# Two moves in the order of one feed-forward pair: the norm's root later on VectorE, the last quarter's turn sooner on TensorE

## The chip, the core and the metric

The kernel runs on one core of a Trainium2 chip. A core has five engines that run beside each other and meet at semaphores: TensorE (PE, and PEld for its weight loads), VectorE (DVE), ScalarE (ACT), GpSimd (POOL) and SyncE (SP), which here only issues DMA. The metric is the device time of one execution in microseconds (us). The median of three runs is 2067.35 us (2067.28 to 2067.61).

## The reference

Two transformer layers stand one behind the other, on 256 rows of width 2048, all in fp32. The change touches the second layer only, where the mixers end and the feed-forward begins:

```python
y = _rms(h, norm_mix_g[i])
z = y @ w_in[i]
...
h = h + jnp.concatenate([oa, ob, oc, od], axis=-1) @ w_out[i]
y = _rms(h, norm_ffn_g[i])
h = h + (jax.nn.silu(y @ w_gate[i]) * (y @ w_up[i])) @ w_down[i]
```

`_rms(x, g)` is `x * rsqrt(mean(x*x) + 1e-6) * g` over a row. The row's factor commutes with the product by the weights, so the kernel multiplies by the gains g first and applies the factor to the sums that come out. The factor is "the norm's root" of this text. D_FF is 5632, which makes 11 blocks of 512 columns of w_gate and w_up, taken as 11 pairs.

## The kernel before, in words

**Products.** Every fp32 matrix is split in a high and a low part, and each product is three matmuls, high by high, low by high, high by low (L714, L715 and L716 in `three`). A *unit* is a block of weights of 128x2048: SyncE loads it to a `raw` buffer, ScalarE copies it to the high part `hi` (L1252, `split`), VectorE makes the low part `lo` by a subtraction (L1721, `split`), and TensorE multiplies. ScalarE and VectorE split unit u + 3 while TensorE is at unit u (AHEAD = 3). There are four `hi` buffers, so ScalarE's split of unit u waits until TensorE has done unit u - 4.

**Residual.** X is the residual stream. The product by w_out of the second layer is four groups, `out2` 0 to 3, each of four units and each for one quarter of X's 512 columns. When a group is done VectorE adds it to its quarter (L2304), ScalarE takes the quarter's sums of squares (L1280 and L1281, counted by `ss3_made`), and TensorE turns the quarter by 8 transposes (L979, `flip`, called by `turn_h`). Of the turned quarter ScalarE writes the high part with the gains (L1268, `high`, four activations) and VectorE the low part (L1822, `low`, four operations). At which unit all this is done for quarter f is said by the table TURN2, which all three engines read.

**The first pair.** The units behind out2 are those of the feed-forward. A pair of 512 columns is done by a scheme with 7 block products for 8 (Strassen's, in Winograd's form), in 11 steps, one unit each, in the order a, x, p2, f, p3, e, d, p0, c, g, p1. BEGIN[0] is the number of the first pair's step a. Steps a, x, f, e, d, c and g are 12 matmuls with 512 columns, and p2, p3, p0 and p1 are 24. The weights of x, f, g and e are no loads: VectorE makes them by subtraction from the loaded blocks (L1738, in `mixed`). Step p2 needs the third quarter turned (`flip_low` to SECOND + 3), and step p3 the last (SECOND + 4). Three rules of order matter here:

- TensorE does the side work of a unit before the unit's matmuls, in order of the program. A transpose that waits holds up all matmuls behind it. The turn of quarter 3 waits for `bank_dve`, which VectorE raises when L2304 of group out2 3 is done.
- VectorE at unit u does first the side work of u (the low part of a turned quarter, the root), then the form and the low part of unit u + 3, then what ends unit u.
- ScalarE at unit u does the side work of u, then the high part of unit u + 3, then what ends unit u; at a step x the copy of a sum (L1504) stands before the high part.

**The root.** From the sums of squares VectorE makes the factor for both halves of the rows: one reduction (L1714), mean and epsilon (L1711), an integer start value (L1688, L1689), three Newton steps of three operations (L1691 to L1693), and two more operations (L2208, L2209) that raise `ffn_scales`. That is 15 operations on 128x2 numbers, each waiting for the one before it. Its first reader is ScalarE's tanh at step p0 (L1526), which waits for `ffn_scales` and for a sum that VectorE adds at the end of step d (L1764, L1766).

Of the kernel before, what the change touches and what calls it, by code (L numbers as in the profile page):

```python
# [241 lines left out]
def build_hybrid(nc, A, C, out, scratch):  # L242
    with ExitStack() as ctx:
# [281 lines left out]
        def freed(name):  # L525

            return named[name].freed
# [35 lines left out]
        OUT, MIXERS, OUT2 = [named[n].first for n in (("out", 0), ("cf", 0), ("out2", 0))]  # L563
# [2 lines left out]
        LAST_GATES = named["gs", GATES - 1].first  # L566
        MERGE = {LAST_GATES + 3: 0, LAST_GATES + 5: 1, OUT: 2, OUT + 1: 3}
        TURN1 = {OUT + 6 + 4 * f: f for f in range(4)}
        TURN2 = {OUT2 + 6 + 4 * f: f for f in range(4)}
        BEGIN = [named["S", j].first for j in range(11)]  # L570
        LAST_DOWN = 4 * LAST_TURN
        TURN3 = {named["down", LAST_DOWN + f].last + 2: f for f in range(4)}
# [43 lines left out]
        def scale_cols(gcol, f):  # L616
            return [VC[:, gcol + 4 * f + k:gcol + 4 * f + k + 1] for k in range(4)]
# [94 lines left out]
        def tensor_program(e):  # L712
# [407 lines left out]
            def turn_h(n, f):  # L1120
                e.wait_ge(flip_low, n)
                flip(lambda t, k: X[:, t, 512 * f + 128 * k:512 * f + 128 * k + 128], 1)
# [12 lines left out]
            def channel_sum(dst, src, counted):  # L1135
                for c in range(4):
                    x = e.matmul(dst, ONE, src[:, c, :], start=c == 0, stop=c == 3)
                x.then_inc(counted, 1)

            def side(u):  # L1140
# [50 lines left out]
                if u == MIXERS + 28:  # L1191
                    e.wait_ge(cv_squared, 1)
                    channel_sum(psB[:, 0, 512:768], CB, channels_summed)
                if u in TURN2:
                    e.wait_ge(bank_dve, freed(("out2", TURN2[u])))
                    turn_h(SECOND + TURN2[u], TURN2[u])
                if u == P_TURN:
# [35 lines left out]
        def scalar_program(e):  # L1233
# [26 lines left out]
            def high(n, dst, pair, scale):  # L1260

                ps = c4(psB[:, pair, :])
                e.wait_ge(flip_turned, turned(n))
                if isinstance(scale, float):
                    e.activation(dst, ps, ACT.Copy, scale=scale).then_inc(flip_high, 1)
                else:
                    for k in range(4):
                        x = e.activation(dst[:, k, :], ps[:, k, :], ACT.Copy, scale=scale[k])  # L1268
                    x.then_inc(flip_high, 1)
# [83 lines left out]
            def part_high(src, block, scale):  # L1353
                e.activation(YH[block], src, ACT.Copy, scale=scale).then_inc(mix_high, 1)

            def side(u):
# [105 lines left out]
                if u == MIXERS + 30:  # L1462
                    e.wait_ge(cn_made, 1)
                    part_high(CA[:, :, :], 2, 0.5)
                if u in TURN2:
                    f = TURN2[u]
                    high(SECOND + f, XH[:, 4 * f:4 * f + 4, :], 1, scale_cols(32, f))
# [209 lines left out]
        def vector_program(e):  # L1677
            steps = [0]

            def finish(x):  # L1680

                steps[0] += 1
                x.then_inc(dve_step, 1)
                e.wait_ge(dve_step, steps[0])

            def rsqrt(v, y, w):
                yi = y.bitcast(I32)
                finish(e.tensor_scalar(yi, v.bitcast(I32), 1, None, ALU.logical_shift_right))  # L1688
                finish(e.tensor_scalar(yi, yi, -1.0, float(0x5F3759DF), ALU.mult, ALU.add))  # L1689
                for _ in range(3):  # L1690
                    finish(e.tensor_tensor(w, y, y, ALU.mult))  # L1691
                    finish(e.scalar_tensor_tensor(out=w, in0=w, scalar=-0.5, in1=v, op0=ALU.mult, op1=ALU.mult))
                    finish(e.scalar_tensor_tensor(out=y, in0=w, scalar=1.5, in1=y, op0=ALU.add, op1=ALU.mult))  # L1693
# [16 lines left out]
            def mean_eps(v, n):  # L1710
                finish(e.tensor_scalar(v, v, 1.0 / n, EPS, ALU.mult, ALU.add))  # L1711

            def row_sums(src, dst):
                finish(e.tensor_reduce(dst, src.rearrange("p (t f) -> p t f", t=2), AX.X, ALU.add))  # L1714
# [98 lines left out]
            def low(n, dst, dstH, pair, scale):  # L1813

                ps, dH = c4(psB[:, pair, :]), dstH.bitcast(F32)
                e.wait_ge(flip_high, n + 1)
                if isinstance(scale, float):
                    e.scalar_tensor_tensor(out=dst, in0=ps, scalar=scale, in1=dH, op0=ALU.mult,
                                           op1=ALU.subtract).then_inc(flip_low, 1)
                else:  # L1820
                    for k in range(4):
                        x = e.scalar_tensor_tensor(out=dst[:, k, :], in0=ps[:, k, :], scalar=scale[k], in1=dH[:, k, :],  # L1822
                                                   op0=ALU.mult, op1=ALU.subtract)
                    x.then_inc(flip_low, 1)
# [219 lines left out]
            def part_low(src, block, scale, n):  # L2044
                e.wait_ge(mix_high, n)
                e.scalar_tensor_tensor(out=YL[block], in0=src, scalar=scale,
                                       in1=YH[block].bitcast(F32), op0=ALU.mult,
                                       op1=ALU.subtract).then_inc(mix_low, 1)
# [20 lines left out]
            def side(u):  # L2069
# [48 lines left out]
                if u in MERGE:  # L2118
                    f = MERGE[u]
# [5 lines left out]
                if u in TURN1:  # L2125
                    f = TURN1[u]
# [63 lines left out]
                if u == MIXERS + 30:  # L2190
# [8 lines left out]
                    part_low(CA[:, :, :], 2, 0.5, 3)  # L2199
                if u in TURN2:  # L2200
                    f = TURN2[u]
                    low(SECOND + f, XL[:, 4 * f:4 * f + 4, :], XH[:, 4 * f:4 * f + 4, :], 1, scale_cols(32, f))
                if u == BEGIN[0] + 3:
                    e.wait_ge(ss3_made, 4)
                    row_sums(ss3, v2)
                    mean_eps(v2, 2048)
                    rsqrt(v2, rr_, w2_)
                    finish(e.tensor_scalar(hr2, rr_, 0.5, None, ALU.mult))  # L2208
                    e.tensor_tensor(r2h, hr2, rr_, ALU.mult).then_inc(ffn_scales, 1)  # L2209
# [10 lines left out]
                if u in TURN3:  # L2220
                    f = TURN3[u]
# [113 lines left out]
            for u in range(n_units):  # L2335
                side(u)
                g, i = units[u]
                if u in ENDED:
                    ended(ENDED[u])
                if 0 < u < n_units - AHEAD:  # L2340
                    if units[u + AHEAD][0].kind == "S":
                        mixed(u + AHEAD)
                    else:
                        split(u + AHEAD)
                if u == GATE_SUMS:
                    e.wait_ge(flip_turned, turned(3))
                    input_forms(GXT, GSS)
                if u == SUMS:
                    e.wait_ge(flip_low, SECOND + 2)
                    input_forms(XT, SS)  # L2350
                if u in FORMS_LOW:
                    forms_low(FORMS_LOW[u])
                if g.kind == "S":
                    gate_up(u)
                elif u == g.last:
                    post(g)
# [95 lines left out]
```

## Time and profile before

| | us |
|---|---|
| median of 3 runs | 2067.35 |
| lowest, highest | 2067.28, 2067.61 |
| the profiled execution | 2066.91 |
| its span, first to last instruction | 2064.8 |
| TensorE busy | 2045.4 (99%) |
| VectorE busy | 1567.9 (76%) |
| ScalarE busy | 1040.9 (50%) |
| granted TensorE clock over the span | 0.998 |

The profiled execution is 2.1 us longer than its span, and 0.4 us under the median. A timeline view has one line for each instruction or row of equal ones: start, duration, engine, line, operation, tiles; in brackets how long the engine had stood idle before it and what released it. Durations on TensorE overlap, since its matmuls are pipelined; what a matmul costs in a row of them is the distance between two starts. The same holds by about 0.08 us for VectorE and ScalarE. In a view of stretches each engine's busy time is followed by its count of instructions; the number behind POOL's is the granted clock, 1.00 for 2.4 GHz and 0.50 for 1.2 GHz.

### The profile page before, as it was taken

The numbers are of one execution on the slowest core, as the hardware profiler recorded it, in microseconds if no ns is written. First come the engines' busy times: TensorE is split into PE (matmuls) and PEld (weight loads), VectorE is DVE, ScalarE is ACT, GpSimd is POOL, SyncE is SP. The second block draws the span as 40 slices with busy tenths as digits, with TensorE's granted clock in tenths as the row PEclk, the third lists the DMA queues.
The fourth block names the chain that finished last, engine by engine and source line by source line (L and its number), as shares of the span: only waits on it lengthen the run. The fifth ranks groups of instructions, "written<-read, shape, count | busy, mean of one in ns | idle before, by whom it ended". The sixth has DMA issues, their size and how long they took to land.

```text
span 2064.8 us, 24955 instructions
## 1 busy us (share of the span) xinstructions
PE 2045.4 (99%) x10311; PEld 1739.1 (84%) x10311; DVE 1567.9 (76%) x1461; ACT 1040.9 (50%) x982; POOL 99.3 (5%) x200
## 2 busy tenths in 40 slices
PE   9999999999999999999999999999999999999998
PEld 8888888888888888888999987888888888888887
DVE  6576555765688888855789859989888889888565
ACT  6444443544455555545344445645455545555453
POOL 2000000000000000000000000111110011110000
PEclk9999999999999999999999999999999999999999
DMA  8655555555565655655655566666566666666461
GB/s 252 215 183 175 166 169 184 164 183 178 189 211 204 222 203 184 219 204 183 210 184 165 182 204 209 230 213 194 192 220 227 211 207 194 201 225 224 145 234 59
DMA packets 229857, 403.61 MB, mean 195 GB/s; under 512 B 13763, under 2 KB 59067, under 8 KB 229489
## 3 DMA queue, kind: packets, MB, share of 16 engines
q1 hardware_dynamic: 221344, 387.64, 56.7%
q0 software_dynamic: 7648, 13.26, 2.2%
q8 instruction: 82, 1.34, 0.3%
q10 hardware_dynamic: 752, 1.12, 0.2%
q14 instruction: 31, 0.25, 0.0%
HBM read 394.62 MB, written 2.12 MB: 192 GB/s over the span
## 4 chain that ended last, share of the span: by engine, by line
PE 89%; DVE 8%; ACT 1%; issue 1%; DMA 1%; ACTq 0%; SPq 0%; DVEq 0%
PE psA L714 20%; PE psA L716 20%; PE psA L715 20%; PE psA L921 6%; PE psB L714 5%; PE psB L715 5%; PE psB L716 5%; PE psA L925 3%; DVE lo L1721 3%; DVE CA L2031 1%; DVE raw L1738 1%; PE psB L979 1%; ACT hi L1252 1%; DVE lo in Y L1721 1%; DMA X<-in_x_dram 0%
## 5 line engine op out<-in xcount | busy, mean ns | idle before, releaser
L1721 DVE TENSOR_TENSOR lo<-raw,hi 128x2048 fp32r<-128x2048 f32 (+2 forms) x364 | 822.7, 2268 | 262.5 <-ACT hi L1252 260.7
L1252 ACT ACTIVATE hi<-raw 128x2048 fp32r<-128x2048 f32 (+2 forms) x364 | 689.2, 1899 | 456.3 <-PE psA L716 300.2
L714 PE MATMUL psA<-hi,XHL 128*128 128x512 f32 x1008 | 393.8, 391 | 1.7 <-DVE XHL L1822 1.7
L716 PE MATMUL psA<-hi,XHL 128*128 128x512 f32 x1008 | 390.9, 388 | 0.0
L715 PE MATMUL psA<-lo,XHL 128*128 128x512 f32 (+1 forms) x872 | 337.7, 387 | 0.0
L714 PE MATMUL psA<-hi,YHL 128*128 128x512 f32 x624 | 244.3, 392 | 0.0
L716 PE MATMUL psA<-hi,YHL 128*128 128x512 f32 x624 | 243.0, 389 | 0.0
L714 PEld LDWEIGHTS psA<-hi,XHL 128*128 128x128 f32 x1008 | 189.4, 188 | 40.9 <-issue 2.1
L716 PEld LDWEIGHTS psA<-hi,XHL 128*128 128x128 f32 x1008 | 189.3, 188 | 39.2
L715 PE MATMUL psA<-lo,YHL 128*128 128x512 f32 x536 | 208.6, 389 | 0.0
L715 PEld LDWEIGHTS psA<-lo,XHL 128*128 128x128 f32 x872 | 163.9, 188 | 32.2
L714 PE MATMUL psA<-XHL,hi 128*128 128x256 f32 (+1 forms) x528 | 150.2, 284 | 1.5 <-DVE lo L1867 1.5
L715 PE MATMUL psA<-XHL,hi 128*128 128x256 f32 (+1 forms) x528 | 149.3, 283 | 0.0
L716 PE MATMUL psA<-XHL,lo 128*128 128x256 f32 (+1 forms) x528 | 149.3, 283 | 0.0
L1252 ACT ACTIVATE hi<-raw in Y 128x2048 fp32r<-128x2048 f32 x55 | 105.5, 1918 | 78.5 <-PE psA L716 48.8
L1721 DVE TENSOR_TENSOR lo in Y<-raw in Y,hi 128x2048 fp32r<-128x2048 f32 x55 | 125.8, 2288 | 24.1 <-ACT hi L1252 23.9
L921 PE MATMUL psA<-XHL,hi 128*128 128x512 f32 x576 | 138.6, 393 | 0.0
L716 PEld LDWEIGHTS psA<-hi,YHL 128*128 128x128 f32 x624 | 117.1, 188 | 24.5
L714 PEld LDWEIGHTS psA<-hi,YHL 128*128 128x128 f32 x624 | 117.2, 188 | 23.9 <-issue 0.3
L921 PEld LDWEIGHTS psA<-XHL,hi 128*128 128x128 f32 x576 | 105.9, 188 | 21.5 <-issue 0.6
L715 PEld LDWEIGHTS psA<-lo,YHL 128*128 128x128 f32 x536 | 100.7, 188 | 20.5
L714 PE MATMUL psB<-hi,XHL 128*128 128x512 f32 (+1 forms) x300 | 115.4, 385 | 1.8 <-DVE lo in Y L1721 1.4
(435 smaller groups left out, 2891.6 us busy)
## 6 DMA issues: line engine op xcount, KB each, us to landing
raw<-in_w_in_dram SPq DMA_DIRECT2D x149, 1024.0 KB, 5.1
raw<-in_w_up_dram SPq DMA_DIRECT2D x35, 1024.0 KB, 5.2
raw<-in_w_gate_dram SPq DMA_DIRECT2D x35, 1024.0 KB, 5.2
raw<-in_w_out_dram SPq DMA_DIRECT2D x32, 1024.0 KB, 5.1
raw<-in_w_down_dram SPq DMA_DIRECT2D x32, 1024.0 KB, 5.1
raw<-in_w_ple_gate_dram SPq DMA_DIRECT2D x14, 1024.0 KB, 5.1
raw<-in_w_branch_dram SPq DMA_DIRECT2D x13, 1024.0 KB, 5.1
raw in Y<-in_w_down_dram SPq DMA_DIRECT2D x12, 1024.0 KB, 5.1
```

Of the source, the lines that this page charges most:

```text
L714: e.matmul(dst, A2[0], B2[0], start=first, stop=False, skip_group_check=True)
L715: e.matmul(dst, A2[0], B2[1], start=False, stop=False, skip_group_check=True)
L716: return e.matmul(dst, A2[1], B2[0], start=False, stop=last, skip_group_check=True)
L921: e.matmul(both, hh[:, s], XHL[:, kb, :, :].rearrange("p a t -> p (a t)"), start=i == 0 and n < 2, stop=False, skip_group_check=True)
L925: x = e.matmul(both[:, 256:512], ll[:, s], XH[:, kb, :], start=False, stop=i == len(g.parts) - 1 and n >= 14, skip_group_check=True)
L979: x = e.transpose(ps[:, k, 128 * t:128 * t + 128], src(t, k), ID[:, :])
L1252: e.activation(hi[u % H][:, 0:m], raw[slot][:, 0:m], ACT.Copy).then_inc(hi_made, 1)
L1721: e.tensor_tensor(lo[slot][:, 0:m], raw[slot][:, 0:m], hi[u % H][:, 0:m].bitcast(F32), ALU.subtract).then_inc(lo_made, 1)
L1738: e.tensor_tensor(of[dst], of[p], of[q], ALU.subtract).then_inc(form_made, 1)
L2031: x = e.scalar_tensor_tensor(out=CA[:, c, :], in0=HP[:, c, j:j + 256], scalar=CW[:, 4 * j + c:4 * j + c + 1], in1=CA[:, c, :], op0=ALU.mul ...
```

## The change

The turn of the last quarter of X stands at unit OUT2 + 17, which is BEGIN[0] + 1 and the first pair's step x; it was at BEGIN[0] + 2, step p2. The other three quarters stay. The root stands at BEGIN[0] + 6, step d; it was at BEGIN[0] + 3, step f.

```diff
-        TURN2 = {OUT2 + 6 + 4 * f: f for f in range(4)}
+        TURN2 = {OUT2 + 6 + 4 * f - f // 3: f for f in range(4)}
...
-                if u == BEGIN[0] + 3:
+                if u == BEGIN[0] + 6:
                     e.wait_ge(ss3_made, 4)
                     row_sums(ss3, v2)
                     mean_eps(v2, 2048)
```

On VectorE, around steps a to f of the first pair. L1822 on XHL is the low part of the turned quarter, L1738 the form that step e uses, L1721 "in Y" the low part for step p3, and L1714 and L1711 begin the root:

```order
 L1721 TENSOR_TENSOR lo<-raw,hi 128x2048
-L1738 TENSOR_TENSOR raw<-raw 128x2048
-L1721 TENSOR_TENSOR lo in Y<-raw in Y,hi 128x2048
 L1822 SCALAR_TENSOR_TENSOR XHL<-psB,VC,XHL 128x256 x4
-L1721 TENSOR_TENSOR lo<-raw,hi 128x2048
+L1738 TENSOR_TENSOR raw<-raw 128x2048
+L1721 TENSOR_TENSOR lo in Y<-raw in Y,hi 128x2048
+L1721 TENSOR_TENSOR lo<-raw,hi 128x2048 x3
+L1721 TENSOR_TENSOR lo in Y<-raw in Y,hi 128x2048
 L1714 TENSOR_REDUCE SM<-SM 128x2
 L1711 TENSOR_SCALAR SM<-SM 128x2
```

The low part of the quarter moved ahead of one form and one low part of weights. Ahead of the root there stand now four low parts of weights behind p3's place (for steps e, d, p0 and c), where one stood.

The root's other end on VectorE, where L2208 and L2209 are its last two operations and L1764 begins what ends step d:

```order
 L2208 TENSOR_SCALAR SM<-SM 128x2
 L2209 TENSOR_TENSOR SM<-SM 128x2
-L1721 TENSOR_TENSOR lo<-raw,hi 128x2048 x2
-L1721 TENSOR_TENSOR lo in Y<-raw in Y,hi 128x2048
 L1721 TENSOR_TENSOR lo<-raw,hi 128x2048
 L1764 TENSOR_TENSOR CG<-CG,SU 128x512
```

The three low parts (steps d, p0 and c) that stood behind the root stand before it; the one that is left is that of step g.

On TensorE, the end of step a, step x (psB from SFH) and the start of step p2 (psA from XHL). L979 x8 is the turn of the last quarter; rows of step x between the two pieces are the same in both:

```order
 L716 MATMUL psA<-hi,XHL 128x512
+L979 MATMUL psB<-ID,X 128x128 x8
 L714 MATMUL psB<-hi,SFH 128x512
 L715 MATMUL psB<-lo,SFH 128x512
...
 L715 MATMUL psB<-lo,SFH 128x512
 L716 MATMUL psB<-hi,SFL 128x512
-L979 MATMUL psB<-ID,X 128x128 x8
 L714 MATMUL psA<-hi,XHL 128x512
 L715 MATMUL psA<-lo,XHL 128x512
```

The turn, and with it its wait for the sum of the last quarter, stands ahead of step x's 12 matmuls instead of behind them. On ScalarE the four L1268 of the quarter stand, in the same way, ahead of the copy of step x's sum (L1504) and one high part instead of behind both. GpSimd's and SyncE's orders are the same.

## Rows read from the trace of the kernel before

**Rows 1.** Chain that ended last, page part 4: share of the span by engine

```profile
PE 89%; DVE 8%; ACT 1%; issue 1%; DMA 1%; ACTq 0%; SPq 0%; DVEq 0%
```

**Rows 2.** Waits of TensorE, whole program: line <- releaser: us, times, longest

```profile
PE psA L714 <- DVE XHL L1822: 1.7, 1, 1.7
PE psB L714 <- DVE lo in Y L1721: 1.4, 2, 0.9
```

**Rows 3.** Timeline, TensorE, 1258 to 1317 us: start, us, form [idle <-releaser]

```profile
1258.44 0.39 PE L716 MATMUL psA<-hi,XHL 128*128 128x512 f32 x1
...
1258.91 0.50 PE L714 MATMUL psB<-hi,SFH 128*128 128x512 f32 x1
...
1262.43 1.09 PE L979 MATMUL psB<-ID,X 128*128 128x128 f32 x8 [0.48 <-DVE X L2304]
...
1263.28 0.47 PE L714 MATMUL psA<-hi,XHL 128*128 128x512 f32 x1
...
1265.90 0.39 PE L716 MATMUL psA<-hi,XHL 128*128 128x512 f32 x1
...
1266.72 0.50 PE L714 MATMUL psB<-hi,XHL 128*128 128x512 f32 x1 [0.43 <-ACT CG L1504]
...
1269.58 0.39 PE L714 MATMUL psA<-hi,SFH 128*128 128x512 f32 x1
...
1272.07 0.39 PE L716 MATMUL psA<-hi,SFL 128*128 128x512 f32 x1
...
1274.14 0.47 PE L714 MATMUL psA<-hi,XHL 128*128 128x512 f32 x1 [1.68 <-DVE XHL L1822]
...
1279.46 0.39 PE L716 MATMUL psB<-hi,XHL 128*128 128x512 f32 x1
...
1316.08 0.50 PE L714 MATMUL psB<-hi,XHL 128*128 128x512 f32 x1 [0.87 <-DVE lo in Y L1721]
```

**Rows 4.** Timeline, VectorE, 1260 to 1286 us

```profile
1260.98 1.40 DVE L2304 SCALAR_TENSOR_TENSOR X<-X,SM,psA 128x512 f32<-128x512 f32 x2
...
1265.73 2.29 DVE L1721 TENSOR_TENSOR lo<-raw,hi 128x2048 fp32r<-128x2048 f32 x1 [1.15 <-ACT hi L1252]
...
1267.94 2.29 DVE L1738 TENSOR_TENSOR raw<-raw 128x2048 f32<-128x2048 f32 x1
...
1272.34 1.65 DVE L1822 SCALAR_TENSOR_TENSOR XHL<-psB,VC,XHL 128x256 fp32r<-128x256 f32 x4
...
1276.11 0.15 DVE L1714 TENSOR_REDUCE SM<-SM 128x2 f32<-128x8 f32 x1
...
1278.95 4.49 DVE L1721 TENSOR_TENSOR lo<-raw,hi 128x2048 fp32r<-128x2048 f32 x2
...
1283.36 2.28 DVE L1721 TENSOR_TENSOR lo in Y<-raw in Y,hi 128x2048 fp32r<-128x2048 f32 x1
...
1285.56 2.28 DVE L1721 TENSOR_TENSOR lo<-raw,hi 128x2048 fp32r<-128x2048 f32 x1
```

**Rows 5.** Timeline, ScalarE, 1265 to 1280 us

```profile
1265.60 0.58 ACT L1497 ACTIVATE S1B<-psA 128x512 f32<-128x512 f32 x1
...
1268.36 1.57 ACT L1268 ACTIVATE XHL<-psB,VC 128x256 fp32r<-128x256 f32 x4
...
1270.26 3.71 ACT L1252 ACTIVATE hi<-raw 128x2048 fp32r<-128x2048 f32 x2 [0.34 <-DVE raw L1738]
...
1279.94 1.92 ACT L1252 ACTIVATE hi<-raw in Y 128x2048 fp32r<-128x2048 f32 x1 [3.67 <-PE psB L716]
```

**Rows 6.** Busy time per engine (instructions), clock, DMA share, GB/s; 1281 to 1315 us

```profile
1281.00:1315.00 34.00, 34.00 (x151) 27.97 (x150) 33.97 (x23) 18.35 (x14) 7.46 (x16) 1.00 0.62 203
```

**Rows 7.** The same view at the program's end

```profile
2055.00:2056.00 1.00, 0.14 (x2) 0.00 (x0) 0.26 (x1) 0.70 (x3) 0.00 (x0) 1.00 1.03 381
...
2057.00:2057.20 0.20, 0.00 (x0) 0.00 (x0) 0.01 (x1) 0.16 (x2) 0.00 (x0) 0.93 0.00 0
...
2057.20:2057.40 0.20, 0.00 (x0) 0.00 (x0) 0.17 (x2) 0.00 (x0) 0.00 (x0) 0.50 0.00 0
```
## The prediction

> **What bounds the kernel now.** I read the chain that ended last first, then TensorE's waits, then the timelines of the engines around the change. The chain is 89% TensorE and 8% VectorE [rows 1]: where TensorE runs without a gap only its own work counts, and the change adds none (the same 8 transposes, the same matmuls). So a difference can only come from the places where TensorE stands idle. Two of the waits of TensorE lie in the stretch that the change reorders [rows 2]: 1.68 us at 1274.14, before step p3, for the low part of the turned quarter, and 0.87 us at 1316.08, before step p3 of the second pair, for a low part of weights [rows 3]. Between 1274.14 and that second wait TensorE does not stop: in 1281 to 1315 both it and VectorE are busy all the time, 34.00 and 33.97 of 34 us [rows 6]. VectorE is the reason of both waits. From 1265.73 on it works back to back (a low part of weights follows another at a distance of 2.20 us: two of them fill 1278.95 to 1283.36 [rows 4]), and it is behind TensorE until 1316. Whatever stops VectorE in 1265 to 1316, or is added to it, is therefore paid by TensorE at 1316. Before 1262.4 nothing of VectorE's order changes.
>
> **The turn, one step sooner: TensorE.** The turn waits for L2304, which ends at 1260.98 + 1.40 = 1262.38 [rows 4]. Its VectorE order up to there is the same, so the turn starts at 1262.43 as before [rows 3]. Step a's last matmul starts at 1258.44; at 0.226 us a matmul (11 steps from 1269.58 to 1272.07) it makes room at 1258.67. Before, step x began at 1258.91 and filled most of the time up to the turn. Now the turn stands ahead of it, and TensorE is idle from 1258.67 to 1262.43, 3.76 us, more than twice the longest wait behind the program's start [rows 2]. Then come the turn (0.85, to 1263.28), step x's 12 matmuls (the first 12 behind a turn took 1263.28 to 1265.90 + 0.23 = 1266.13), and then p2 and f, 36 matmuls at 0.2264 = 8.15 us. So TensorE is at p3 at 1274.28. In between it waited 0.43 for ScalarE's copy of x's sum before [rows 3]; now that copy comes behind the four L1268: L1497 begins at 1265.60 and leaves ScalarE at about 1266.1, the four take 1.57, to 1267.7 [rows 5], the copy, like L1497, 0.58, to 1268.3. The second half of p2 needs it at 1266.13 + 12 x 0.2264 = 1268.85, so that wait is gone. p3 starts at 1274.28 for 1274.14: the turn's place alone gives back its own gap and costs 0.1 us, as long as the clock stays.
>
> **The turn: VectorE.** The low part of the quarter (distance 1.57 from 1272.34) and the form and the low part that change places with it (2.20 each) add up to the same: 1267.94 + 1.57 + 2.20 + 2.20 = 1273.91, as before [rows 4]. The quarter's high part, ready at 1267.7, is just in time for 1267.94. The form now ends at 1271.8 for 1270.2, and ScalarE's next high part waits for it [rows 5]: 1271.8 + 1.90 = 1273.7, 0.2 ahead of VectorE's need at 1273.91. So p3's operands are all there at 1274.0, as before, and TensorE's 1274.28 decides. The 1.68 us wait isn't saved, it has become part of the 3.76.
>
> **The root, three steps later.** Its 15 operations take 1276.11 to 1278.95, 2.84 us [rows 4]. Without it there VectorE does the low parts of d and p0 at 1276.11 and 1278.31 (their high parts: ScalarE ends them at 1273.7 + 1.86 = 1275.6 and, behind a copy, 0.58 + 1.90 later, at 1278.1) and is free at 1280.52. Next is the low part of step c. Its high part takes a buffer that step p3 holds, and ScalarE began it at 1279.94, when p3 had ended (last matmul started at 1279.46 [rows 3, 5]). Now p3 is continuous with f and its last matmul starts at 1274.28 + 23 x 0.2264 = 1279.49, so nothing has come sooner: high part 1279.97 to 1281.89, low part from 1281.91. VectorE is idle for 1281.91 - 1280.52 = 1.39 us. Before, the root stood in just this time, and c's low part began at 1283.36. Then: c's low part to 1284.11, root to 1286.95, and g's low part starts at 1286.95 for 1285.56, **1.39 us late**. From there to 1316 VectorE has no idle time in which to win it back [rows 6], and TensorE's wait there (0.87) grows by it; a part may fall one step sooner. The other reader of the root, the tanh of p0, waits for L1766 anyway, which is behind the root in either order; it gets late by the same 1.39, and its sum is used by VectorE only at step g, three TensorE steps on. SyncE's loads that wait for x, p2 and f are issued later by as much as these steps end later, x most: 1266.13 for 1258.91 + 12 x 0.227 = 1261.6, 4.5 us. None of the waits shown in this stretch is for a load [rows 3 to 5], so I cost them at nothing; without that cover it would be up to the 4.5.
>
> **The clock.** Rows show at the program's end what idle TensorE does to its clock: the last matmul ended at 2055.14 (0.14 us busy in 2055 to 2056), and at 2057.17 (0.93 is the mean over 2057.00 to 2057.20) the granted clock fell from 1.00 to 0.50, that is from 2.4 to 1.2 GHz, 2.03 us behind it [rows 7]. The idle 1.68 us at 1274 didn't make it fall, the mean over 1281 to 1315 is 1.00 [rows 6]. The new gap of 3.76 us is longer than either. I take it that the clock falls in it or just behind it. No row has matmuls at the low level, so the price is bounded: 0 if it doesn't fall, and if it stays low through the turn, x, p2 and f (0.85 + 2.85 + 8.15 = 11.85 us) another 11.9. The row nearest is the fall after 2.03 us; if the low level then lasts about as long as the gap that made it, 3.76 us, between 2.03 us (fall early) and 3.76 us (fall at the gap's end) of work is done at half speed, which adds 1.0 to 1.9. I take 1.3. TensorE's 1274.28 decides for p3, so that this passes on to the high part of c, to VectorE's idle time and to 1316 in full.
>
> The Trainium skill ("TensorE: Matmul & The Clock Gate", "HAM oscillation — how this bites in real kernels") says that a TensorE which idles too long between its matmuls is set back to the low clock and starts cold again. The end of this trace agrees, with the fall 2.03 us behind the last matmul; no run here yet shows it in the middle of the work. By the page the sum is the forecast's; without it, it is that of the first rival, 2068.7.
>
> **Sum.** Against the profiled execution, 2066.91: idle VectorE 1.39, clock 1.3 (p3's later end is in the 1.39 already): +2.7, 2069.6. The median is 0.44 higher: **2070.0 us**, 0.13% slower. This is under 0.2%, about what a measurement of this kernel tells from no change.
>
> **Rivals.**
> - *The clock stays.* Only the root's term is left, 2067.35 + 1.4 = 2068.7. For it: the clock was kept through the 1.68 us. Against it: the fall after 2.03 us.
> - *Not slower: p3's wait is saved.* If VectorE had any idle time between 1265.73 and 1273.99 that the new order fills, p3 starts sooner, by at most the 1.68 us that TensorE waited; then c's high part comes 1.7 us sooner as well, VectorE's new idle time (1.39) vanishes, and the time is down to 2067.35 - 1.7 = 2065.7. It decides from 0.3 us on, since below that TensorE's own arrival is last. Against it stand the back-to-back rows 4, and TensorE's count, which has 48 matmuls to do behind 1263.28.
> - *Slower by over 0.2%: the clock stays low.* From 2.8 us lost by it the sum passes 4.1. That is more than 5.5 us of work at the low level; if it lasts to p3, 2067.35 + 1.4 + 11.9 = 2080.6. For it: the end row stays at 0.50 from its fall on; against it: TensorE is idle there.
> - *The moves don't do what they say* has no room: both orders show the rows moved.
>
> **Chances.** Forecast 0.60, clock stays 0.26, saved wait 0.08, clock low for long 0.06. The forecast alone reaches from 2069.2 to 2071.2 (clock 0.5 to 2.4). For 8 in 10 the range must take in the first rival: 2068.0 to 2071.6. Faster by over 0.2% (under 2063.2) is beyond every case, 0.01. Slower by over 0.2% (over 2071.5) is the last rival and the forecast's edge, 0.06. Within 0.2%: 0.93.
>
> **What would show it.** In the changed kernel's timeline: TensorE idle for 3.7 to 3.8 us before L979, released by L2304; no wait for L1504's copy; p3 starting 11.0 us behind the turn's end if the clock stays at 1.00, and 12.3 if it falls, with a stretch under 1.00 and matmuls about twice as far apart in step x. VectorE idle for 1.4 us, or 2.7 with the fall, before "lo in Y" of step c, released by ScalarE, and the root's 15 operations behind it. TensorE's wait before the second pair's p3 at 2.3 us or so, or shared with the step before. From there on both traces run alike, shifted by one number. The prediction is wrong if g's low part isn't late, or if the wait at 1316 hasn't grown.

## The result

| | before | changed |
|---|---|---|
| median, us | 2067.19 | 2070.14 |
| lowest, highest | 2066.48, 2067.72 | 2069.39, 2070.98 |
| runs | 20 | 20 |
| ratio | | 1.0015 (95%: 1.0009 to 1.0021) |
| span of the profiled execution | 2064.8 | 2068.1 |

The changed kernel is 2.95 us slower. The interval excludes no change, and the size is under the 0.2% that the prediction named.

The change can't move the start of L2304, the sum of the last quarter, but it is at 1260.98 us before and at 1261.25 in the changed kernel, and between 1260.51 and 1261.85 in the eleven profiled executions of this study. So all positions below are counted from it. The measure that sums up the stretch is the distance from there to the start of the second pair's p3: 1316.08 - 1260.98 = 55.10 us before [rows 3, 4]. Behind that p3 nothing differs: from it to the end of the span it is 748.6 to 748.7 us in all eleven.

TensorE of the changed kernel, rows that answer to rows 3 (start, duration, form, idle time ahead and what released it):

```profile
1258.72 0.39 PE L716 MATMUL psA<-hi,XHL 128*128 128x512 f32 x1
...
1262.71 1.27 PE L979 MATMUL psB<-ID,X 128*128 128x128 f32 x8 [3.60 <-DVE X L2304]
...
1265.05 0.63 PE L714 MATMUL psB<-hi,SFH 128*128 128x512 f32 x1
...
1265.48 0.63 PE L715 MATMUL psB<-lo,SFH 128*128 128x512 f32 x1
...
1276.17 0.39 PE L714 MATMUL psA<-hi,XHL 128*128 128x512 f32 x1
...
1281.39 0.39 PE L716 MATMUL psB<-hi,XHL 128*128 128x512 f32 x1
...
1314.99 0.50 PE L714 MATMUL psA<-hi,SFH 128*128 128x512 f32 x1 [0.58 <-DVE lo L1721]
...
1319.40 0.50 PE L714 MATMUL psB<-hi,XHL 128*128 128x512 f32 x1 [1.38 <-DVE lo in Y L1721]
```

TensorE is idle for 3.60 us ahead of the turn, released by L2304; step x's matmuls stand at a distance of 0.43 us at first (1265.05 to 1265.48), for 0.23 before; p3 starts at 1276.17, 14.92 us behind L2304's start, for 13.16. The wait ahead of the second pair's p3 is 1.38 us, and 0.58 us more stand one step sooner. Its start is 58.15 us behind L2304's: 3.05 us more than before.

The granted clock in that stretch (busy time per engine with counts, clock, DMA share, GB/s):

```profile
1263.00:1263.50 0.50, 0.50 (x7) 0.50 (x6) 0.50 (x1) 0.47 (x3) 0.00 (x0) 0.99 0.98 381
...
1263.50:1266.50 3.00, 3.00 (x10) 2.42 (x9) 1.85 (x2) 3.00 (x5) 0.00 (x0) 0.50 0.05 17
...
1266.50:1267.00 0.50, 0.50 (x3) 0.41 (x2) 0.50 (x1) 0.50 (x2) 0.00 (x0) 0.60 0.00 0
```

It falls to 0.50 (1.2 GHz) at 1263.50, 0.8 us behind the end of the idle time, and is back at 1.00 (2.4 GHz) at 1266.90 (0.60 is the mean of the last stretch's 0.5 us): 3.4 us at the low level, from the last of the transposes over most of step x.

VectorE, rows that answer to rows 4:

```profile
1261.25 1.40 DVE L2304 SCALAR_TENSOR_TENSOR X<-X,SM,psA 128x512 f32<-128x512 f32 x2
...
1268.21 1.65 DVE L1822 SCALAR_TENSOR_TENSOR XHL<-psB,VC,XHL 128x256 fp32r<-128x256 f32 x4
...
1283.82 2.29 DVE L1721 TENSOR_TENSOR lo in Y<-raw in Y,hi 128x2048 fp32r<-128x2048 f32 x1 [2.72 <-ACT hi L1252]
...
1286.03 0.15 DVE L1714 TENSOR_REDUCE SM<-SM 128x2 f32<-128x8 f32 x1
...
1288.88 2.29 DVE L1721 TENSOR_TENSOR lo<-raw,hi 128x2048 fp32r<-128x2048 f32 x1
```

VectorE is idle for 2.72 us ahead of the low part of step c, then come that part, the root (1286.03 to 1288.88) and step g's low part, 27.63 us behind L2304 for 24.58 before (1285.56 [rows 4]): 3.05 us late. The same number arrives at the second pair's p3.

ScalarE, rows that answer to rows 5:

```profile
1266.35 1.56 ACT L1268 ACTIVATE XHL<-psB,VC 128x256 fp32r<-128x256 f32 x4
...
1268.19 0.60 ACT L1504 ACTIVATE CG<-psB 128x512 f32<-128x512 f32 x1 [0.28 <-PE psB L716]
...
1281.87 1.92 ACT L1252 ACTIVATE hi<-raw in Y 128x2048 fp32r<-128x2048 f32 x1 [3.10 <-PE psB L716]
```

The quarter's high part ends at 1267.91, 0.3 us ahead of VectorE's low part at 1268.21. The high part of step c waits for TensorE's p3 (last matmul at 1281.39) and starts at 1281.87.

### The profile page after: what moved, and what is told of

It reads as the page before. It is cut to its first block and busy times, and to the rows that moved or that the text cites. A ratio compares the mean times of both kernels' runs of the same rounds, so it can differ in the third digit from the quotient of the medians.

```text
span 2068.1 us, 24955 instructions
## 1 busy us (share of the span) xinstructions
PE 2048.4 (99%) x10311; PEld 1741.9 (84%) x10311; DVE 1568.1 (76%) x1461; ACT 1040.8 (50%) x982; POOL 99.3 (5%) x200
## 5 line engine op out<-in xcount | busy, mean ns | idle before, releaser
L1721 DVE TENSOR_TENSOR lo<-raw,hi 128x2048 fp32r<-128x2048 f32 (+2 forms) x364 | 822.6, 2268 | 262.0 <-ACT hi L1252 260.1
L1721 DVE TENSOR_TENSOR lo in Y<-raw in Y,hi 128x2048 fp32r<-128x2048 f32 x55 | 125.8, 2288 | 26.8 <-ACT hi L1252 26.6
```

Source lines behind the costliest of these rows:

```text
L1721: e.tensor_tensor(lo[slot][:, 0:m], raw[slot][:, 0:m], hi[u % H][:, 0:m].bitcast(F32), ALU.subtract).then_inc(lo_made, 1)
```

## The experiments

Each is told by its distance from L2304 to the second pair's p3, from one profiled execution, and by its median beside that of the kernel before on the same chip. Where the clock stays high the distance is good to some 0.05 us (56.52 and 56.52, 55.10 and 55.11 below); the medians scatter by a few tenths (2068.30 and 2068.77 for the same 56.52). Where the clock falls, one execution need not stand for all: see the kernel with the root at step e. Of the kernels made for this study only the last one's interval excludes no change; the distances and the waits carry the argument.

| kernel | p3 of first pair | p3 of second pair | against before | median, before beside it |
|---|---|---|---|---|
| before | 13.16 | 55.10 | | |
| changed | 14.92 | 58.15 | +3.05 | 2070.14, 2067.19 |
| turn only | 14.81 | 56.14 | +1.04 | 2068.25, 2067.13 |
| root only | 13.16 | 56.52 | +1.42 | 2068.30, 2067.13 |
| changed, gap filled | 13.29 | 56.52 | +1.42 | 2068.77, 2067.13 |
| turn only, gap filled | 13.30 | 55.11 | +0.01 | 2066.75, 2066.74 |
| changed, root at step e | 16.02 | 57.35 | +2.25 | 2068.07, 2067.13 |
| changed, gap filled by half | 14.90 | 58.13 | +3.03 | 2070.79 (one run) |
| root in two parts | 13.23 | 54.66 | -0.44 | 2066.00, 2067.16 |
| form early | 11.92 | 53.87 | -1.23 | 2065.58, 2067.16 |
| form early, root on GpSimd | 11.93 | 53.36 | -1.74 | 2064.69, 2067.16 |

**The turn alone.**

```diff
-        TURN2 = {OUT2 + 6 + 4 * f: f for f in range(4)}
+        TURN2 = {OUT2 + 6 + 4 * f - f // 3: f for f in range(4)}
```

> Only the turn of the last quarter is one step sooner; the root stays at step f. Theory (two terms that meet at VectorE): TensorE idle 3.6 to 3.8 us before the turn, the clock falls, and p3 of the first pair starts 1.6 us later than before. But VectorE has the root to do in that time: its low part for step c starts only 0.2 us later (high part ready at 1283.5 for 1283.36), so most of the 1.6 us is absorbed, and at the second pair's p3 TensorE's own arrival (1315.05 + 1.6 - 0.1 = 1316.6 for 1316.08) decides: +0.5 to +0.6 us, 2067.8. Rival (the clock's loss is paid in full wherever the root stands): +1.6 us, 2068.8. Rival (the clock did nothing): 0.0.

TensorE, VectorE and the clock of this kernel; L2304 started at 1260.65:

```profile
1275.46 0.39 PE L714 MATMUL psA<-hi,XHL 128*128 128x512 f32 x1
...
1316.79 0.50 PE L714 MATMUL psB<-hi,XHL 128*128 128x512 f32 x1 [0.36 <-DVE lo in Y L1721]
```

```profile
1283.11 2.29 DVE L1721 TENSOR_TENSOR lo in Y<-raw in Y,hi 128x2048 fp32r<-128x2048 f32 x1
...
1286.26 2.29 DVE L1721 TENSOR_TENSOR lo<-raw,hi 128x2048 fp32r<-128x2048 f32 x1 [0.85 <-ACT hi L1252]
```

```profile
1261.50:1262.00 0.50, 0.00 (x0) 0.00 (x0) 0.50 (x2) 0.00 (x0) 0.00 (x0) 0.88 1.04 406
...
1265.00:1265.50 0.50, 0.50 (x3) 0.36 (x3) 0.11 (x1) 0.50 (x2) 0.00 (x0) 0.71 0.00 0
```

ScalarE's high part of step g, in the kernel before and in this one:

```profile
1283.10 1.91 ACT L1252 ACTIVATE hi<-raw 128x2048 fp32r<-128x2048 f32 x1
```

```profile
1284.32 1.91 ACT L1252 ACTIVATE hi<-raw 128x2048 fp32r<-128x2048 f32 x1
```

p3 is 1.65 us late (14.81 for 13.16), and step c's low part only 0.08 (22.46 behind L2304 for 22.38): the root covers the wait, as expected. But the end is +1.04, between both theories. What I had left out stands in VectorE's last row: step g's low part waits another 0.85 us for ScalarE, whose high part of g stands behind the copy of step e's sum, which TensorE's delay has moved too. Before, that high part ended at 1285.01, 0.55 us ahead of its reader (1285.56 [rows 4]); now it is 1.55 us later against L2304. So g's part is 1.03 us late, and that is what is paid at 1316. The root covers the clock's loss at step c in full, and only some 0.6 us of it at step g.

**The root alone.**

```diff
-                if u == BEGIN[0] + 3:
+                if u == BEGIN[0] + 6:
```

> Only the root is three steps later; the turn stays at step p2. Theory: VectorE idle 1.3 to 1.4 us before the low part of step c, which waits for a buffer that TensorE's p3 holds; everything from step g's low part on 1.4 us late; the wait before the second pair's p3 grows from 0.87 to 2.2 us, or part of it moves to the step before; clock 1.00 throughout; +1.4 us, 2068.6. Rival (the whole difference comes from the turn and its clock): 0.0, 2067.2.

VectorE; L2304 started at 1261.00:

```profile
1281.94 2.29 DVE L1721 TENSOR_TENSOR lo in Y<-raw in Y,hi 128x2048 fp32r<-128x2048 f32 x1 [1.32 <-ACT hi L1252]
...
1287.00 2.28 DVE L1721 TENSOR_TENSOR lo<-raw,hi 128x2048 fp32r<-128x2048 f32 x1
```

1.32 us of idle time ahead of step c's low part, released by ScalarE; g's low part 26.00 us behind L2304 for 24.58, 1.42 late; +1.42 at the end, with p3 of the first pair untouched. The theory stands, and the rival (all of it is the clock) falls.

**The changed kernel with its gap filled.** 15 matmuls that nobody reads stand ahead of the turn's wait.

```diff
                 if u in TURN2:
+                    if TURN2[u] == 3:
+                        e.wait_ge(flip_low, SECOND + 3)
+                        for _ in range(15):
+                            e.matmul(psB[:, 1, 0:512], XH[:, 0, 0:128], XHL[:, 1, :, :].rearrange("p a t -> p (a t)"),
+                                     start=True, stop=True, skip_group_check=True)
                     e.wait_ge(bank_dve, freed(("out2", TURN2[u])))
```

> The changed kernel with 15 matmuls of 128x512 put ahead of the turn's wait for the last quarter; they write the bank that the turn overwrites, from operands that are long ready, and nobody reads them. TensorE is then idle for 0.3 to 0.4 us instead of 3.6. Theory: the granted clock stays at 1.00, p3 starts as before (1274.3 on the clock of before), and only the root's 1.4 us are left: 2068.6. Rival (it is the order of turn and step x that costs, not the clock): still +3.0 us, 2070.1.

TensorE:

```profile
1259.39 3.56 PE L1198 MATMUL psB<-XHL 128*128 128x512 f32 x15
...
1263.16 1.09 PE L979 MATMUL psB<-ID,X 128*128 128x128 f32 x8 [0.21 <-DVE X L2309]
...
1275.00 0.39 PE L714 MATMUL psA<-hi,XHL 128*128 128x512 f32 x1
...
1318.23 0.50 PE L714 MATMUL psB<-hi,XHL 128*128 128x512 f32 x1 [1.39 <-DVE lo in Y L1726]
```

The wait for L2304 is 0.21 us, the granted clock 1.00 over 1259 to 1280, p3 13.29 us behind L2304, where the prediction's sum without the clock had 13.30 (1274.28 - 1260.98). The end is at +1.42, the very distance of the root alone: turn, order and waits are the changed kernel's, only the idle time is gone, and with it 1.63 us. The clock is the cause of that part.

**The turn alone, gap filled.** Both edits above, with the root at its old place.

> Only the turn of the last quarter one step sooner (root at step f, as before), with the 15 matmuls of 128x512 ahead of its wait that nobody reads. Theory (the turn's place costs by the clock alone): clock 1.00 throughout, p3 13.3 us behind the start of the sum of the last quarter for 13.16, second pair's p3 not more than 0.1 us late: 0.0 to +0.1 us, 2067.2. Rival (the turn's place costs by its order too): +1.0, as with the turn alone.

TensorE, the second pair's p3; L2304 started at 1260.85 here (1315.96 - 1260.85 = 55.11):

```profile
1315.96 0.50 PE L714 MATMUL psB<-hi,XHL 128*128 128x512 f32 x1 [0.85 <-DVE lo in Y L1726]
```

+0.01 us. With the four kernels the two causes are separate: the root's place costs 1.41 with the clock high (gap filled, +0.01 against +1.42), and 2.01 with it low (+1.04 against +3.05). The difference of 0.60 us is what was absorbed of the clock's loss with the root at its old place.

**The changed kernel with the root at step e.**

```diff
-                if u == BEGIN[0] + 6:
+                if u == BEGIN[0] + 5:
```

> The changed kernel with the root one step sooner, at step e (unit 5) instead of d: it then stands in VectorE's order just ahead of step c's low part, in the idle time that waits for p3's buffer. Theory: VectorE's new idle time goes to 0.1 us, the clock still falls, and what is left is that of the turn alone, +0.5 to +0.6 us, 2067.8. Rival (the root's late end delays the gates' tanh and by that TensorE): still about +3 us, 2070.1. Rival (the clock's loss is paid in full): +1.6, 2068.8.

The clock of the profiled execution:

```profile
1261.00:1261.50 0.50, 0.00 (x0) 0.00 (x0) 0.50 (x1) 0.00 (x0) 0.00 (x0) 0.80 0.92 356
...
1261.50:1268.00 6.50, 5.68 (x18) 4.82 (x19) 5.36 (x5) 5.19 (x10) 0.00 (x0) 0.50 0.28 107
...
1268.00:1268.50 0.50, 0.50 (x4) 0.41 (x3) 0.50 (x2) 0.00 (x0) 0.00 (x0) 0.87 0.00 0
```

The low level lasted from 1261.30 to 1268.13, twice as long as in the changed kernel, and p3 was 2.7 us late instead of 1.6 (against 13.29). So the distance, +2.25, can't be held against +1.04. The 11 executions can: they fall in two groups, six from 2067.66 to 2068.07 with a mean clock of 0.998 and five from 2068.71 to 2069.13 with 0.997, and the profiled one (2069.1) is of the second. The turn alone has seven from 2067.55 to 2068.36 at 0.998, the profiled one (2067.68, low level 3.4 us) among them, and four from 2068.89 to 2069.09 at 0.997. That the second groups are those of the long low level is likely, and not shown but for the one profile. The medians of the first groups are 2067.85 here and 2067.98 for the turn alone, 0.7 and 0.9 above before: with the root at step e the turn's cost is left, as the theory had it. The rival of a late tanh (2070.1) falls by it, and so does that of a loss paid in full (2068.8), by these groups alone.

**The changed kernel with the gap half filled:** 7 matmuls instead of 15.

> The changed kernel with 7 matmuls of 128x512 instead of 15 put ahead of the turn's wait: they take 1.6 to 1.8 us, and TensorE is idle for about 2.0 us before the turn. Theory: with the granted clock falling whenever TensorE is idle for some 2 us, as at the program's end, p3 starts up to 1.6 us late and the time is +1.4 to +3.0; if this gap is already short enough to keep the clock, p3 starts as in the kernel with the full 15 and +1.4 is left. No rival separates here; the run says on which side 2.0 us lies in one execution.

```profile
1259.53 1.75 PE L1198 MATMUL psB<-XHL 128*128 128x512 f32 x7
...
1263.31 1.20 PE L979 MATMUL psB<-ID,X 128*128 128x128 f32 x8 [2.03 <-DVE X L2309]
```

```profile
1264.00:1264.50 0.50, 0.50 (x5) 0.50 (x4) 0.50 (x1) 0.47 (x2) 0.00 (x0) 0.67 0.53 201
...
1264.50:1267.50 3.00, 3.00 (x9) 2.32 (x8) 1.85 (x2) 3.00 (x6) 0.00 (x0) 0.50 0.00 0
...
1267.50:1268.00 0.50, 0.50 (x3) 0.42 (x3) 0.50 (x1) 0.50 (x2) 0.00 (x0) 0.92 0.00 0
```

A gap of 2.03 us was enough in this execution, and the clock fell at 1264.17, 0.9 us after TensorE had begun to work again, to 1267.58. The end is +3.03, as in the changed kernel. It is one execution.

**The root in two parts.** Its first five operations are called behind the form in step f's `mixed`, the other ten stay.

```diff
                     form("g", "c", "f")
+                    if g.name == ("S", 0):
+                        root_begin()
```

> The kernel before with the root cut in two: its first 5 operations (reduction, mean, start value, first square) go between the form and the low part of step f, where VectorE stands idle for 1.15 us (it waits for ScalarE's high part); the other 10 stay at step f's side work. Theory (in 1265 to 1316 VectorE's idle time decides, and what fills it is won at the second pair's p3): the 5 operations cost 1.0 us of idle time, everything from there on is 1.0 us sooner on VectorE, the wait of 0.87 us goes and TensorE's own arrival (1315.05 for 1316.08) decides: -0.9 to -1.0 us, 2066.2. Rival (VectorE's order doesn't matter as long as its work is the same): 0.0.

```profile
1316.29 0.50 PE L714 MATMUL psB<-hi,XHL 128*128 128x512 f32 x1 [0.37 <-DVE lo in Y L1737]
```

```profile
1266.45 2.29 DVE L1737 TENSOR_TENSOR lo<-raw,hi 128x2048 fp32r<-128x2048 f32 x1 [0.34 <-ACT hi L1252]
...
1285.76 2.29 DVE L1737 TENSOR_TENSOR lo<-raw,hi 128x2048 fp32r<-128x2048 f32 x1 [0.39 <-ACT hi L1252]
```

The wait ahead of step f's low part went from 1.15 to 0.34 us, and step c's low part is 0.92 us sooner against L2304 (21.46 for 22.38). But at step g's low part a new wait of 0.39 stands, released by ScalarE, as in the kernel with the turn alone; it is 0.45 sooner (24.13 for 24.58), and p3 0.44, for the -0.9 to -1.0 expected. Half of the gain is lost there: the expectation had left out the same term. The median is 1.2 under before (2066.00), but 0.4 of that lies outside the span, 1.8 us here for 2.1 to 2.2 before, and the median of the spans is 0.8 under before. The rival (0.0) is off; the size is open between 0.4 and 0.8.

**The form early.** The form for step e is made right behind the form for step g, in the idle time, instead of at p3.

```diff
                     form("g", "c", "f")
+                    if g.name == ("S", 0):
+                        form("b", "d", "b")
...
-                elif role == "p3":
+                elif role == "p3" and g.name != ("S", 0):
                     form("b", "d", "b")
```

> The kernel before with the form for step e (L1738 'raw<-raw') made ahead of step f's low part, in VectorE's 1.15 us idle time, instead of at p3. Theory: lo of f from 1266.75 (TensorE needs it at 1269.6), p3's low part and the turned quarter's low part both 1.1 us sooner, p3 starts at 1272.8 for 1274.14, all of VectorE 1.1 to 1.2 us sooner up to 1316: second pair's p3 at 1314.9 for 1316.08, -1.2 us, 2066.0. Rival (as for the split root): 0.0. Rival (p3's gain counts alone, VectorE is not the bound at 1316): -1.4.

L2304 (L2306 in this kernel) started at 1260.51.

```profile
1264.02 2.29 DVE L1738 TENSOR_TENSOR raw<-raw 128x2048 f32<-128x2048 f32 x1
...
1266.23 2.29 DVE L1721 TENSOR_TENSOR lo<-raw,hi 128x2048 fp32r<-128x2048 f32 x1
```

```profile
1272.43 0.47 PE L714 MATMUL psA<-hi,XHL 128*128 128x512 f32 x1 [0.45 <-DVE XHL L1824]
...
1314.38 0.50 PE L714 MATMUL psB<-hi,XHL 128*128 128x512 f32 x1 [0.90 <-DVE lo in Y L1721]
```

No idle time is left ahead of step f's low part, p3 starts 11.92 us behind L2304 for 13.16, and the end is -1.23 us for -1.2 expected; step g's low part (1283.86) is 1.23 sooner too. The rival of 0.0 is off. That of -1.4 is not told apart by the number, since p3 of the first pair is itself 1.24 sooner and the median is 1.6 under before; what speaks against it is the wait of 0.90 us, which still stands at the end and is VectorE's. The term is VectorE's idle time of 1.15.

**The form early and the root on GpSimd.** The root's operations, 19 here, stand in GpSimd's program ahead of its first move of hidden values.

```diff
+            e.wait_ge(ss3_made, 4)
...
+            finish(e.tensor_tensor(v2, s8[:, :, 0], s8[:, :, 1], ALU.add))
...
+            finish(e.tensor_scalar(yi, v2.bitcast(I32), -0.5, float(0x5F3759DF), ALU.mult, ALU.add))
+            for _ in range(3):
+                finish(e.tensor_tensor(w2_, rr_, rr_, ALU.mult))
+                finish(e.tensor_tensor(w2_, w2_, v2, ALU.mult))
+                finish(e.tensor_scalar(w2_, w2_, -0.5, 1.5, ALU.mult, ALU.add))
+                finish(e.tensor_tensor(rr_, rr_, w2_, ALU.mult))
...
+            e.tensor_tensor(r2h, hr2, rr_, ALU.mult).then_inc(ffn_scales, 1)
```

> As the kernel with the early form, and the root is made by GpSimd, which is free from 1257 to 1306 (its own start value by one multiply-add of the integer, three Newton steps of four operations, 20 operations in all; VectorE waits for ffn_scales before the first use). Theory: VectorE loses 2.84 us of work, but then waits for ScalarE's high parts of c and g, which TensorE paces: g's low part at 1283.7 for 1285.56, second pair's p3 at 1314.2: -1.8 to -1.9 us, 2065.3. Rival (TensorE's pace is all that is left from p3 on): -1.4. Rival (GpSimd's small operations are so slow, or disturb VectorE so much, that the root is late at p0, 1289): slower than before.

TensorE, VectorE and GpSimd:

```profile
1314.69 0.50 PE L738 MATMUL psB<-hi,XHL 128*128 128x512 f32 x1 [0.36 <-DVE lo in Y L1745]
```

```profile
1261.33 1.40 DVE L2325 SCALAR_TENSOR_TENSOR X<-X,SM,psA 128x512 f32<-128x512 f32 x2
...
1271.45 1.66 DVE L1848 SCALAR_TENSOR_TENSOR XHL<-psB,VC,XHL 128x256 fp32r<-128x256 f32 x4
...
1273.02 6.69 DVE L1745 TENSOR_TENSOR lo<-raw,hi 128x2048 fp32r<-128x2048 f32 x3
...
1281.01 2.29 DVE L1745 TENSOR_TENSOR lo in Y<-raw in Y,hi 128x2048 fp32r<-128x2048 f32 x1 [1.30 <-ACT hi L1276]
...
1284.16 2.29 DVE L1745 TENSOR_TENSOR lo<-raw,hi 128x2048 fp32r<-128x2048 f32 x1 [0.85 <-ACT hi L1276]
```

```profile
1264.33 7.26 POOL L716 TENSOR_TENSOR SM<-SM 128x2 f32<-128x2 f32 x1 [6.87 <-ACT psB L1305]
...
1273.06 6.71 POOL L723 TENSOR_TENSOR SM<-SM 128x2 f32<-128x2 f32 x1
...
1281.23 2.13 POOL L725 TENSOR_TENSOR SM<-SM 128x2 f32<-128x2 f32 x1
...
1284.27 2.23 POOL L725 TENSOR_TENSOR SM<-SM 128x2 f32<-128x2 f32 x1
...
1287.22 0.19 POOL L727 TENSOR_TENSOR SM<-SM 128x2 f32<-128x2 f32 x1
```

-1.74 us for -1.8 to -1.9 expected. The median, 2064.69 us, is 2.5 under the kernel before (ratio 0.9989, 95%: 0.9980 to 0.9998), of which 0.4 lies outside the span, as with the root in two parts. It is 5.4 under the changed kernel. VectorE lost 2.84 us of work and got back 1.30 and 0.85 us of waiting for ScalarE's high parts of c and g: behind p3 TensorE's pace bounds, as the theory said. GpSimd ended the root at 1287.4, in time: p0's tanh came at 1287.81, held up by a sum of VectorE.

## Why the prediction was right

- **The bound.** Right. What VectorE was late or early at step g's low part was paid or won at the second pair's p3 one to one (3.05 and 3.05; 1.42 and 1.42; 1.03 and 1.04; -1.23 and -1.23; -1.75 and -1.74).
- **The turn on TensorE.** Right. The gap was 3.60 us by the row and 3.76 as predicted when it is counted from the last matmul's slot (1258.72 + 0.23 to 1262.71), the wait for ScalarE's copy is gone, and without the clock p3 came at 13.29 us for 13.30 worked out.
- **The turn on VectorE and ScalarE.** Right: the quarter's high part was 0.3 us ahead of its reader, and the high part that waits for the form 0.2 us ahead of its own.
- **The root.** 1.42 us measured, 1.39 worked out.
- **The clock.** Right in its mechanism, and mis-sized: 1.63 us for the 1.3 taken (bounds 1.0 to 1.9). The step assumed a low level that lasts as long as the gap, 3.76 us; it lasted 3.4 in the changed kernel and 6.8 in the one with the root at step e. It began 0.8 us behind the gap and not in it, so that all of it met work, where the 1.3 had it begin partly inside. Twice the time per matmul (0.43 for 0.23) holds.
- **That it passes on in full.** Right for the changed kernel. What made it so is the root's new place: with the root at its old one 0.6 of 1.6 us were absorbed. The prediction added the two terms and didn't say that they depend on each other.
- **SyncE's loads.** Nothing waited for them.
- **The sum.** 2.7 us predicted, 2.95 by the medians, 3.05 by the distance, 2070.0 for 2070.14.
- **Rivals.** The clock stayed high in no profiled execution with the gap, and in 20 runs the fastest (2069.39) is slower than the slowest of 11 with the gap filled (2069.18), which makes it likely that it fell in all. A saved p3 wait didn't happen: VectorE had no idle time there for the new order to fill. The same idea with the idle time that exists, the 1.15 us ahead, gained 1.23. A low level for over 5.5 us was profiled once, with the root at step e: 6.8 us, of which 1.0 met idle time, for 2.7 us at p3. By times and mean clocks it is likely in 5 of 11 executions there and in 4 of 11 of the turn alone, more often than a chance of 0.06 says, but at 2.7 us it costs just less than the 2.8 from which the rival begins. The rival's price of 11.9 us didn't occur.

The Trainium skill ("TensorE: Matmul & The Clock Gate", "HAM oscillation — how this bites in real kernels") speaks of gaps in the midst of work that set the clock back, and of the cold start behind them. The trace agrees: 3.60 us of idle time, then 3.4 us at 0.50.

## What to carry to other kernels

An operation that waits should stand behind the work that its engine can do meanwhile: moving the turn ahead of step x saved none of the wait and made one idle stretch of 3.60 us out of three (0.48, 0.43 and 1.68 us), long enough to lower TensorE's clock. Small work that fills an engine's wait is free where it stands; before moving it, look which wait it covers and what paces that wait (here a buffer held by TensorE's p3). And the profitable move is the reverse, to look for idle time upstream of the late engine (1.15 us here) and put into it what stands in the way downstream.

## What the runs showed of the hardware

- The granted clock fell to 0.50 after idle stretches of TensorE of 3.60 us (0.8 us after work had begun again), 3.61 and 3.62 us (inside the gap, 0.2 and 1.0 us before its end) and 2.03 us (0.9 us after work had begun again). It didn't fall at 1.72 us, at the wait before p3 in the kernel with the split root. The low level lasted 3.4 us three times and 6.8 us once, so that the price of a gap of 3.6 us ranged from 1.5 to 2.7 us at p3. A gap of 2.03 us cost 1.6, in one execution.
- GpSimd's operations on 128x2 numbers take 0.2 us, but one took 7.26, one 6.71, one 2.23 and one 2.13 us. Each ended with VectorE's subtractions of two SBUF tensors: the first at 1271.59, at the end of four of them and the start of L1848, which reads PSUM (1271.45); the second at 1279.77, at the end of the three low parts (1279.71), behind which VectorE stood idle; the other two at 1283.36 and 1286.50, at the end of one low part each (1283.30 and 1286.45). The Trainium skill ("SBUF — State Buffer", section "SBUF: two separate sides") says of the port pair that the two share that the one blocks the other for a whole instruction when VectorE's has two SBUF inputs. The trace agrees, and shows that a row of back-to-back VectorE instructions keeps GpSimd out for more than one.
